# The gated MLP of a two-block kernel in two stages: all up units, the products to DRAM, then the down-projection by token halves with eight tiles in PSUM

## The reference

```
def conv_mlp(h, w_up, conv_w, w_down):
    u = dwconv3(h @ w_up, conv_w)          # 1024 -> 2 * 2816, depthwise width-3 convolution over tokens
    gate, val = jnp.split(u, 2, axis=-1)
    return (jax.nn.silu(gate) * val) @ w_down

x = x + rmsnorm(y_mixer, norm_mix_post)
h = rmsnorm(x, norm_ffn_pre)
y = conv_mlp(h, w_up, conv_ffn, w_down)
x = x + rmsnorm(y, norm_ffn_post)
h = rms_norm(x, l0_norm)                   # the second block begins with h @ l0_w_in
```

## Time and profile before

| | us |
|---|---|
| median of three runs (1938.01 to 1939.05) | 1938.3 |
| the profiled execution | 1938.83 |
| its span, first to last instruction | 1937.0 |
| PE busy in the span (8516 matmul records) | 1846.2 |
| DVE busy | 1193.7 |
| POOL busy | 731.9 |
| ACT busy | 548.5 |
| mean granted TensorE clock, share of full | 0.982 |

### The profile page before, as it was taken

How to read it: one execution, slowest core, us unless ns; L and a number is a source line. 1 busy time by engine, 2 the same in 40 slices (tenths; PEclk the granted TensorE clock), 3 DMA queues, 4 the chain that set the end, 5 groups by cost and what they waited for, 6 DMA issues and landing times.

```text
span 1937.0 us, 21432 instructions
## 1 busy us (share of the span) xinstructions
PE 1846.2 (95%) x8516; PEld 1503.9 (78%) x8516; DVE 1193.7 (62%) x1171; ACT 548.5 (28%) x653; POOL 731.9 (38%) x304
## 2 busy tenths in 40 slices
PE   6998999999999999999999999799999999999996
PEld 5777877877688888888888887578778888888785
DVE  6354666743986575567567655792756666666534
ACT  4332222222520000000000000431345556566521
POOL 5446554364134445445443644234421010101052
PEclk9999988999999999999999999899999999999998
DMA  4323222122411111112111111332211010111232
GB/s 159 109 98 98 76 76 66 33 66 84 155 44 46 42 55 53 46 32 65 43 43 43 54 54 59 121 117 74 87 60 44 20 36 33 43 33 66 82 120 87
DMA packets 44452, 131.90 MB, mean 68 GB/s; under 512 B 5056, under 2 KB 5440, under 8 KB 44384
## 3 DMA queue, kind: packets, MB, share of 16 engines
q1 hardware_dynamic: 30800, 94.91, 15.8%
q10 hardware_dynamic: 13584, 36.02, 5.0%
HBM read 104.18 MB, written 26.74 MB: 68 GB/s over the span
## 4 chain that ended last, share of the span: by engine, by line
PE 77%; DVE 13%; issue 4%; ACT 3%; POOL 2%; DMA 0%; DVEq 0%; ACTq 0%; POOLq 0%; SPq 0%
PE psum L522 49%; PE psum L868 5%; PE psum L889 5%; PE psum L826 4%; PE psum L925 4%; PE psum L878 2%; PE psum L546 2%; DVE cc L1619 1%; PE psum L851 1%; DVE spv L1522 1%; DVE ptl L1739 1%; PE psum L667 1%; DVE yo L1584 1%; DVE rstd L1411 1%; DVE yo L1644 1%
## 5 line engine op out<-in xcount | busy, mean ns | idle before, releaser
L394 POOL TENSOR_TENSOR wh<-wstage,ones 128x1024 fp32r<-128x1024 f32 x122 | 299.2, 2452 | 956.4 <-PE psum L522 561.4
L522 PE MATMUL psum<-hh,wh 128*128 128x512 f32 x1200 | 378.9, 397 | 23.1 <-POOL wl L397 20.6
L522 PE MATMUL psum<-hl,wh 128*128 128x512 f32 x1200 | 372.2, 392 | 0.0
L522 PE MATMUL psum<-hh,wl 128*128 128x512 f32 x1200 | 371.3, 391 | 0.0
L397 POOL TENSOR_TENSOR wl<-wstage,wh 128x1024 fp32r<-128x1024 f32 x122 | 323.4, 2651 | 9.6
L522 PEld LDWEIGHTS psum<-hh,wh 128*128 128x128 f32 x1200 | 224.7, 189 | 76.3 <-issue 24.6
L522 PEld LDWEIGHTS psum<-hl,wh 128*128 128x128 f32 x1200 | 227.1, 189 | 47.8
L522 PEld LDWEIGHTS psum<-hh,wl 128*128 128x128 f32 x1200 | 226.7, 189 | 47.7
L1619 DVE SCALAR_TENSOR_TENSOR cc<-uu,col,cc 128x1023 f32<-128x1023 f32 x88 | 176.8, 2009 | 9.0 <-DVE cc L1613 0.6
L1420 DVE TENSOR_TENSOR uu<-psum,rstd 128x1024 f32<-128x1024 f32 x44 | 53.7, 1222 | 141.2 <-PE psum L522 141.2
L1644 DVE TENSOR_TENSOR yo<-yo,psum 128x1024 f32<-128x1024 f32 x80 | 97.3, 1217 | 57.1 <-PE psum L522 57.1
(11 more groups left out here) (276 smaller groups left out, 3191.5 us busy)
## 6 DMA issues: line engine op xcount, KB each, us to landing
wstage<-w_units SPq DMA_DIRECT2D x133, 512.0 KB, 3.5
resid<-yo SPq DMA_DIRECT2D x32, 256.0 KB, 2.1
mix<-spill ACTq DMA_DIRECT2D x12, 512.0 KB, 2.6
xin<-xT ACTq DMA_DIRECT2D x8, 512.0 KB, 8.5
kq<-mix SPq DMA_DIRECT2D x16, 256.0 KB, 3.9
gates<-gspill ACTq DMA_DIRECT2D x8, 512.0 KB, 2.6
rstd<-gates ACTq DMA_DIRECT2D x16, 256.0 KB, 2.8
res<-resid ACTq DMA_DIRECT2D x8, 512.0 KB, 7.8
```

What stands on the lines that cost most here:

```text
L394: pool.tensor_tensor(high, wstage[:, s], ones[:, :].unsqueeze(1).to_broadcast([P, 8, P]), ALU.mult).then_inc(w_high, 1)
L522: mm = pe.matmul(out[:, t], w[:, wslot, b, :], x[part][:, xk, t], start=start and n == 0, stop=stop and n == 2)
```

## The change

The up units and the down units are no longer interleaved. First PE does all 44 up units (the first four by halves, as before), with four slots in turn. The product of each pair is not split but stored by ACT to a DRAM tensor `acts` (512 KB for each of 22 pairs); DVE's code and ACT's are written out for the 22 pairs instead of looped.

Then the down-projection runs by halves of the tokens. For each half, the 22 pairs follow one another; in a step, one pair's tile of 512 tokens is multiplied with one down unit for all eight output tiles, 24 matmuls, each tile having a PSUM bank of its own in which it adds up over all 22 steps. So the tiles are taken out of PSUM once for each half, by ACT (even tiles) and DVE (odd ones), instead of being added onto `yo` eleven times. The down units are loaded and split twice, once for each half: 22 units more (NU is 155 instead of 133). Their high parts are made by ACT, their low parts by POOL, in a ring of five places (DEEP = 5); the tiles of `acts` are loaded by SP into five buffers `ain`, ACT makes the high and DVE the low parts.

The second half's steps 0 to 2 leave out tile 7, whose bank holds the sums of squares of the first half, and make it up after step 2. The residual stage of the first half (8 tiles) is put between the steps of the second half. The first halves of the next block's first four units come straight after the last down step, and the sum of squares of the second half after the first of them. The eight instructions that zeroed `yo` go, and so do POOL's additions of squares.

```diff
-U_LOOP = U_FF + 4
-U_L0 = 99
-U_ATT = 113
-U_LAST = 125
-NU = 133
-
-BY_ACT = (*range(U_FF + 3, U_FF + 9), *range(U_L0 + 1, U_L0 + 5))
+U_DOWN = U_FF + 2 * FT
+U_L0 = U_DOWN + 2 * FT
+U_ATT = U_L0 + 14
+U_LAST = U_ATT + 12
+NU = U_LAST + 8
+
+DEEP = 5
+BY_ACT = (*range(U_FF + 3, U_FF + 9), *range(U_DOWN, U_L0 + 5))
...
+        acts = nc.dram_tensor("acts", (FT, P, T), F32, kind="Internal").ap()
...
+        cc, uu = over(("cc", [P, 3, T], F32), ("uu", [P, 2, T], F32))
...
-        ah, al, cc, uu = over(("ah", [P, 4, T], F32R), ("al", [P, 4, T], F32R), ("cc", [P, 2, T], F32),
-                              ("uu", [P, 2, T], F32))
+        ah, al, ain = over(("ah", [P, DEEP, HT], F32R), ("al", [P, DEEP, HT], F32R), ("ain", [P, DEEP, HT], F32))
...
+        DEEP_PLACES = (EXTRA[0], EXTRA[1], in_slot(1), in_slot(2), in_slot(0))
+
+        def place(u):
+
+            if U_DOWN <= u < U_L0 + 4:
+                return DEEP_PLACES[(u - U_DOWN) % DEEP]
+            if u < U_FF + 1 or u >= U_L0 + 4:
+                return in_slot(u % RING)
+            return EXTRA[0] if u == U_FF + 1 else in_slot((u + 2) % RING)
...
+            if u in (U_L0 + 5, U_L0 + 6):
+                return U_L0 + (3 if u == U_L0 + 5 else 4)
+            return u - RING + 1
 
 
         def halves_before(n, half):
@@ -187,7 +216,7 @@
...
+            def move_residual(n, half, k, source, dest):
+                t = slice(half * HT, half * HT + HT)
+                sync.wait_ge(res_ready, halves_before(n, half) + k + 1)
+                sync.dma_start(dest[k, :, t], yo[:, k, t]).then_inc(res_out, DMA)
+                if k + 2 < KT:
+                    sync.dma_start(xr[:, k % 2, t], source[k + 2, :, t]).then_inc(xr_in[k % 2][half], DMA)
+
+            def load_activation(i):
+
+                half, p = i // FT, i % FT
+                t = slice(half * HT, half * HT + HT)
+                if half == 0:
+                    sync.wait_ge(act_out[p % 2], DMA * (p // 2 + 1))
+                if i >= DEEP:
+                    sync.wait_ge(a_lo, i - DEEP + 1)
+                sync.dma_start(ain[:, i % DEEP], acts[p, :, t]).then_inc(tile_in[i % DEEP], DMA)
+
...
+                        load_unit(U_FF + 5)
+                    move_residual(1, half, k, xT, resid1)
+            for u in range(U_FF + 6, U_DOWN):
+                load_unit(u)
+            for i in range(2 * FT):
+                load_activation(i)
+                load_unit(U_DOWN + i)
+                if FT + 9 <= i < FT + 9 + KT:
+                    move_residual(2, 0, i - FT - 9, resid1, resid2)
+            for u in range(U_L0, U_L0 + 7):
+                load_unit(u)
+            for k in range(KT):
...
+            pool.wait_ge(h_lo, 2 * KT)
+            split_one(U_FF + 3)
+            pool.wait_ge(h_lo, 3 * KT)
+            for u in range(U_FF + 4, U_L0 + 4):
...
-            for u in range(U_L0 + 3, U_L0 + 5):
-                pool.wait_ge(h_lo, (u - U_L0 + 1) * KT)
-                low_part(u, in_slot(u % RING))
-            for u in range(U_L0 + 5, (U_L0 // 6 + 2) * 6):
...
-            def down(base, buf, groups, wslot=(U_LOOP + 6) % RING):
-
-                pe.wait_ge(w_split, base + 2)
-                pe.wait_ge(a_lo, groups * 2 + 2)
-                for m in range(KT):
-                    if not isinstance(groups, int) or groups or m >= 2:
-                        pe.wait_ge(down_evac, groups * KT + (m - 1))
-                    for kk in range(2):
-                        mm = products(slot(2 + m % 2), (wslot + kk) % RING, m, (ah, al), 2 * buf + kk,
-                                      kk == 0, kk == 1)
-                    if m < KT - 1:
+            def ff_unit(j, count):
+
+                pe.wait_ge(w_split, count + (U_FF + 1))
+                pe.wait_ge(up_evac, count - 3)
+                unit(slot(j % 4), (U_FF + j + 2) % RING, H)
+
+            with pe.Fori(0, 3) as i:
+                for j in range(4, 16):
+                    ff_unit(j, i * 12 + j)
+            for j in range(40, 2 * FT):
+                ff_unit(j, j)
+
+            def down(half, k, tiles):
+
...
+                i = half * FT + k
+                high, low = DEEP_PLACES[i % DEEP]
+                for m in tiles:
+                    for n, (w, x) in enumerate(((high, ah), (high, al), (low, ah))):
+                        mm = pe.matmul(bank(m), w[:, m, :], x[:, i % DEEP, :], start=k == 0 and n == 0,
+                                       stop=k == FT - 1 and n == 2)
+                    if m == KT - 1:
+                        mm.then_inc(unit_done, 1)
+                    elif k == FT - 1:
                         mm.then_inc(down_done, 1)
+
+            for half in range(2):
+                for k in range(FT):
+                    pe.wait_ge(w_split, U_DOWN + half * FT + k + 1)
+                    pe.wait_ge(a_lo, half * FT + k + 1)
+                    if k:
+                        down(half, k, range(KT - 1) if half and k < 3 else range(KT))
                     else:
-                        mm.then_inc(unit_done, 2)
-
-            def ff_group(i, d, first):
-
-                base = i * 12 + (U_LOOP + 6 * d)
-                for j in range(4):
-                    pe.wait_ge(w_split, base + (j + 1))
-
-                    pe.wait_ge(up_evac, j + 1 if first and j < 2 else i * 8 + (4 * (1 + d) + j - 1))
-                    unit(slot(j % 2), (U_LOOP + 2 + j) % RING, H)
-                down(base + 4, d % 2, i * 2 + d)
-
-            ff_group(0, 0, True)
-            ff_group(0, 1, False)
-            with pe.Fori(1, 5) as i:
-                ff_group(i, 0, False)
-                ff_group(i, 1, False)
...
+            FIRST_L0 = [place(U_L0 + j) for j in range(4)]
+            pe.wait_ge(y_odd, 4 + 1)
+            norm_sum_half(2, 0, 1)
+            for j in range(4):
+                pe.wait_ge(w_split, U_L0 + j + 1)
+                pe.wait_ge(y_even, 4 + j + 1)
+                for k in range(KT):
+                    half_products(bank(2 * j), FIRST_L0[j], k, 0, k == 0, k == KT - 1)
+                if j == 0:
+                    pe.wait_ge(y_odd, 8)
+                    sum_half(1, 7, (acc_step, KT - 1 + 12), (fsq_ready, 2 * KT))
+            pe.wait_ge(root_ready, 4)
+            for k in range(KT):
+                pe.wait_ge(h_lo, KT + halves_before(2, 1) + k + 1)
+                for j in range(3):
+                    mm = half_products(bank(2 * j + 1), FIRST_L0[j], k, 1, k == 0, k == KT - 1)
+                    if k == KT - 1:
+                        mm.then_inc(unit_done, 1)
+            pe.wait_ge(half_root, 4)
+            norm_sum_half(2, 1, 7)
+            pe.wait_ge(root_ready, 5)
+            for k in range(KT):
+                mm = half_products(bank(7), FIRST_L0[3], k, 1, k == 0, k == KT - 1)
+            mm.then_inc(unit_done, 1)
+
             for j in range(4, len(L0_SLOTS)):
...
+            def ff_silu(p):
 
                 act.wait_ge(tap_sum, p * 6 + 3)
                 act.activation(cc[:, 0, :], cc[:, 0, :], ACT.Silu).then_inc(act_silu, 1)
+
+            def ff_store(p):
                 act.wait_ge(a_mul, p + 1)
-                act.activation(ah[:, b, :], cc[:, 1, :], ACT.Copy).then_inc(a_hi, 1)
...
+            def down_parts(i):
+
+                weight_high(U_DOWN + i)
+                act.wait_ge(tile_in[i % DEEP], DMA * (i // DEEP + 2))
+                if i >= DEEP:
+                    act.wait_ge(unit_done, U_DOWN + i - DEEP + 1)
+                act.activation(ah[:, i % DEEP], ain[:, i % DEEP], ACT.Copy).then_inc(a_hi, 1)
+
+            weight_high(U_FF + 6)
+            for p in range(FT):
+                ff_silu(p)
+                if p < 2:
+                    weight_high(U_FF + 7 + p)
+                ff_store(p)
+                if p >= FT - 3:
+                    for i in ((0, 1), (2, 3), (4,))[p - FT + 3]:
+                        down_parts(i)
             act.wait_ge(res_out, 2 * KT * DMA)
...
+                def taken(m):
+                    act.wait_ge(*((down_done, half * (KT - 1) + m + 1)))
+                    act.activation(yo[:, m, t], bank(m), ACT.Copy).then_inc(y_even, 1)
+
+                def squared(m):
+                    if m % 2:
+                        act.wait_ge(y_odd, half * 4 + m // 2 + 1)
+                    else:
+                        act.wait_ge(y_even, half * 4 + m // 2 + 1)
+                    if m >= 3:
+                        act.wait_ge(acc_step, KT - 1 + half * 6 + m - 2)
+                    act.activation(sq[:, m % 2, t] if m else root[:, t], yo[:, m, t], ACT.Square).then_inc(fsq_ready, 1)
+
+                taken(0)
+                squared(0)
+                taken(2)
+                squared(1)
+                taken(4)
+                squared(2)
...
+            for i in range(DEEP, FT + 4):
+                down_parts(i)
+            down_tiles(0)
+            down_parts(FT + 4)
+            half_roots(0, KT - 1, 3)
+            for i in range(FT + 5, FT + 8):
```

(52 more changed lines are left out.)

415 lines of the change are left out of this document (153 added, 262 removed).

## The result

The changed kernel takes **1904.67 us** (median of four runs, 1903.03 to 1906.10) against 1938.49 before: 33.8 us or 1.75% less, ratio 0.9825 with a 95% interval of 0.9808 to 0.9842. The forecast was 1900.0 in a range of 1897.5 to 1912, so the time lies in the range, 4.7 us above the point. The profiled execution took 1903.62 us, 35.2 less than the profiled one before.

What follows compares the result with a forecast made beforehand. PE was taken to bound the kernel, with 39.9 us lost in the rewritten stretch; 1.4 would remain, a gain of 38.5, taking the span from 1937.0 to 1898.5 and the time to about 1900 us, range 1897.5 to 1912.

Steps and rivals of the forecast that it cites:

- What is lost before the change: Rewritten stretch: 725.1 us needed, 765.0 spent, 39.9 lost in the ten groups, last down step and next block's first units.
- Up units, down steps, staging: Up units 40 x 10.88 = 435.3 us; down steps 239.4 us; a staging turn 7.5 us against 10.9 available.
- The rival of the weights: Down steps bound by weight loads if landing exceeds 6.9 us instead of 3.5; 1935 at 8.5 us landing; chance 0.05.
- The rule against it: Down steps: cycling PSUM banks could drop PE's clock to 1.2 GHz; 2005 us if half run so; rival's chance 0.03.
- a down step: Each step 5.44 us of PE, beside ACT 1.06 + about 0.65, POOL 2.63 and DVE about 0.7.
- between the halves: First half's tiles and squares taken out in time; eight residual half tiles, 20.0 us of DVE beside about 100 of PE, free.
- The end: After the last down step E: no waits for hl, one new wait of 0.8 us, stretch ending at E + 49.5.
- about 1 us: Behind the stretch, DVE empties the first two slots that much before PE needs them; costed at nothing.
- needed at 17.1: Behind the stretch: second slot empty 15.8 us after the sums' end, PE needing it at 17.1.
- the joints cost: Rival: one of three fits of 1.0 to 1.4 us fails or the squares are slower; 1903 to 1914; chance 0.15.
- 1898 to 1903 held at 0.73: Likeliest case: the time comes out as in the sum, in us; chance 0.73.
- Everything behind as long as before, 637 us: Sign for the profile: what follows the rewritten stretch keeps its length of 637 us.

Runs made afterwards that it cites:

- experiment 4: Kernel before the change, interleaving kept, only VectorE's additions onto yo moved to other places between its taps; 1927.06 us, ratio 0.9941.
- experiment 3: Changed kernel with the first half's residual stage after the last down step instead of between the second half's steps; 1919.04 us, ratio to before 0.9900.
- Experiment 6: Changed kernel with the high parts of the 22 down units made by GpSimd instead of ScalarE; 1929.25 us, ratio to before 0.9947.
- experiment 5: Changed kernel with GpSimd waiting to split the seventh L0 unit until the rope key's low part is made; 1900.66 us, one run.
- experiment 1: Changed kernel with ScalarE making a down tile's high part before the weight's high part; 1904.5 us, one run.
- experiment 2: Changed kernel with ScalarE making the step's parts before the residual tile in the eight steps that carry one; 1904.31 us, one run.
- Experiment 7: Changed kernel with tile's high part first, GpSimd held until the rope key's low part, and the fourth gate tile taken out behind the third; 1895.34 us.
- Experiment 8: The changed kernel unchanged, run again in a later set; 1901.77 us, ratio to before 0.9814.

## Why the prediction was right, and where it was short

**What is lost before the change** was right. The 39.9 us were placed as 10.8, 16.7 and 12.3. The first is shown by experiment 4: 11.0. What the interleaving of the residual stage is worth is shown by experiment 3: 14.4, near to the 12.3 of the next block's first units plus the waits that follow when they are late. The last down step's share, 16.7, has no experiment of its own; what is left for it is 33.8 - 11.0 - 14.4 = 8.4 us and whatever the new joints cost, and how much of it the two others overlap stays open.

**Up units, down steps, staging** were right. 435.3 us were said and measured. 239.4 were said for the down steps and 241.4 measured, 239.9 without the wait of 1.5 for al; loads land in 3.6 and 3.9 us. The rival of the weights did not come. Experiment 6 shows, though, that the room was less than its 3.4 us suggested: GpSimd could do its part for PE, but not without taking VectorE's.

**The rule against it** did not come true. PE changed bank after every third of 1056 matmuls at a clock of 1.00. By the section of the Trainium skill cited in the prediction the down steps might have run partly at the lower clock; the trace does not agree. In the down stage the clock fell in experiment 6 alone (0.98 and 0.96), where PE stood still three times for 4.5 to 5.3 us; in experiment 3 it fell just behind the last down step (0.95 from 1195 to 1216 us), after a stop of 3.9.

**The step that failed** is in "a down step" and "between the halves": *DVE about 0.7* for the low part, and the eight residual tiles that *cost nothing* as 20.0 us of DVE beside 100 us of PE. The term was taken from rows, beside which POOL mostly stood idle (9.6 us of work in 59.3), and put into steps in which it works nearly half of the time (56 us in 129). The low part measured 2.35 us on average, and the residual tiles came one every 7.18 us, 57 us for eight instead of 20, still within the 100 but out of step with the tiles that PE wanted next. The prediction had seen that work beside POOL's is longer, but only as an argument for a rival, "against" which it set the room of 1 us. The Trainium skill ("SBUF — State Buffer", section "Who interferes with whom") says it in a rule: a VectorE instruction with two inputs in SBUF contends with a GpSimd instruction that reads SBUF, and whoever issues first holds the shared port for its whole instruction. The rows agree: 0.69 against 2.48 us for the same 44 instructions, 1.22 against 3.33 for the rope product (experiment 5); out of PSUM (L1451), with one input in SBUF, 1.22 us each whatever POOL does. The 3.49 against 7.88 for three subtractions agree with one engine standing behind the other, but not with the order of starts: GpSimd's began first both times. Price in this stretch: a wait of 1.5 us, and the stretch is 2.1 shorter without it (experiments 1 and 2).

**The end** failed by as little. The two fits by *about 1 us* were worked out with rows of before. There POOL was beside one instruction of this chain, the low part of the key (L1697, 3.04 us), and the four rope instructions took 1.22 each. In the changed kernel POOL is beside two of the rope instructions (3.3 each, 4.2 us more), and the low part takes 1.22 (1.8 less): 2.4 us more where the room was 1.3, and *needed at 17.1* was missed by 0.9 us; experiment 5 shows that POOL is the cause. That is the rival "the joints cost", which had 0.15 and 1903 to 1914: its mechanism came beside the 37 us won: for 0.9 us at a fit that it named, and for the 1.5 of al at a place that it did not. The time of 1904.67 lies in its range and not in the 1898 to 1903 held at 0.73; the second set of runs of the same kernel, 1901.77, lies in the latter. So the wide range held, and which of the two cases the time falls in is within the scatter between sets.

**"Everything behind as long as before, 637 us"** was 640.2. Besides the 0.9, PE's old wait for the gate tile (2.58 us at 1356.03, at 1392.84 before) is now followed by slow matmuls:

```profile
1356.03 0.70 PE L521 MATMUL psum<-hh,wh 128*128 128x512 f32 x2 [2.58 <-DVE gspill L1451]
...
1357.61 1.05 PE L521 MATMUL psum<-hh,wh 128*128 128x512 f32 x2
1358.46 1.05 PE L521 MATMUL psum<-hl,wh 128*128 128x512 f32 x2
1359.32 1.05 PE L521 MATMUL psum<-hh,wl 128*128 128x512 f32 x2
```

Each row stands for two matmuls, 0.85 us apart instead of 0.45, the lower of the two clocks (1.2 GHz); with the rows at either end it is 1.6 us. In the kernel before and in experiment 5 the same wait is followed by the full pace, so the fall is not certain after such a wait. Experiment 7 takes the wait away, and no slow matmuls follow there. Experiment 8, the same kernel, has neither, and is 635.7 us long behind the stretch: the 637 forecast lies between the two executions.

The account of the profiled executions: 38.5 forecast; less 1.5 in the stretch, less 0.9, 1.6 and 0.4 behind it (the 0.4 I can't place), plus 1.15 upstream: 35.2 (within rounding). The 1.15 can't be put down to the change, since in the profiles of the changed kernel and of experiments 3 and 5, which have the same code there, the stretch begins between 533.1 and 533.5 us, and in experiment 8 at 536.1. The median gained 33.8; the 1.4 between are the scatter of the four runs. Experiment 7 gets 43.0 us, more than the 39.9 that the forecast called the most that can be won, because it also removes a wait behind the stretch that was already there.

## What to carry to other kernels

A duration read where the neighbouring engine was idle is a lower bound for the place to which the work is moved. For each VectorE instruction with both inputs in SBUF, look at what GpSimd does at that moment, and cost it with the rest of GpSimd's instruction if it starts behind it. Where the two must share a step, the order on the engine that starts them both decides: swapping two of ScalarE's lines made the stretch 2.1 us shorter. Count the room of an engine together with what its busy time does to its neighbour: GpSimd had time for the high parts, and giving them to it cost 27 us. And profile a kernel more than once before putting a microsecond down to an edit.

## What the runs showed of the hardware

- VectorE's 128x512 subtraction or scalar_tensor_tensor from SBUF: 0.68 to 0.74 us alone, 2.46 to 2.88 when it starts 0.5 us behind a 128x1024 instruction of GpSimd, 1.35 when it starts 1.6 behind (experiment 1). The cost is not a slower rate but the rest of the other's instruction; GpSimd's own becomes longer where both start together (1261.88: 3.47 us, alone 2.40).
- A VectorE COPY of 128x1024 does the same with one input: 0.69 us in experiment 5 (1270.37), 2.81 in the changed kernel (1284.93) behind a 2.39 us instruction of GpSimd.
- When GpSimd's instruction begins 0.3 us before VectorE's, either can be the one that stands: 7.88 us for VectorE and 2.62 for GpSimd, or 3.49 and 6.05.
- VectorE's share of the page (63% in the changed kernel, 61% in experiment 7, same instructions) contains such waiting: 45 us of 1196.8 are gone in experiment 7, with no work removed, 41 of them by the edit of experiment 1 alone.
- After a wait of PE of 2.6 us for the same gate tile the clock fell in four executions (the changed kernel's first, experiments 1, 2 and 3: matmuls 0.43 us apart for some 3 us) and not in three (the kernel before, experiments 5 and 6).
- The clock falls at other places from run to run: two more short falls upstream go with a start of the stretch 3 us later in experiments 1, 2 and 8, as much as the effects measured there. Lengths of stretches told them apart; total times of single runs did not.
